# Another order for a program's opening: tables, norm rows and the first token tile ahead of the weight work

## What is computed

```python
def rms_norm(x, g):
    y = x * rsqrt(mean(x * x, axis=-1, keepdims=True) + EPS)
    return y * g
def swiglu(x, w_in, w_out):                # d_model 1024, d_ff 2816
    gate, up = split(x @ w_in, 2, axis=-1)
    return (silu(gate) * up) @ w_out
h = swiglu(rms_norm(x, g[0]), w_ffn_in[0, 0], w_ffn_out[0, 0])
x = x + 0.5 * rms_norm(h, g[1])
...
ATTN_PATTERNS = ((128, 1), (512, 4), (2048, 16))   # window, dilation: allowed distances
```

## Time and profile before

| | |
|---|---|
| median of 3 executions | 1462.7 us (1462.68 to 1465.63) |
| the profiled execution | time 1466.29 us, span 1464.4 us |
| granted TensorE clock, mean | 0.979 |
| TensorE products busy | 1389.5 us, 95% of the span |
| VectorE, ScalarE, GpSimd busy | 495.7, 659.1, 1037.0 us |
| DMA | 246.94 MB, mean 169 GB/s |

### The profile page before, as it was taken

The page is one execution under the profiler, slowest core; times in us unless marked ns, Lnnn a source line. Parts: engine busy times, 40 slices in busy tenths (PEclk is TensorE's granted clock), DMA queues, the critical chain, the costliest instruction groups (busy, mean ns, idle before and its releaser), DMA issues.

```text
span 1464.4 us, 17488 instructions
## 1 busy us (share of the span) xinstructions
PE 1389.5 (95%) x6396; PEld 1136.8 (78%) x6396; DVE 495.7 (34%) x1108; ACT 659.1 (45%) x760; POOL 1037.0 (71%) x241
## 2 busy tenths in 40 slices
PE   6799999989999999999999789999999999989997
PEld 4588888777888878888887567888878777778786
DVE  5610124565110156211003675110156133572235
ACT  5344435436444445544434556343455443544531
POOL 5778885818978866888887408978866966658763
PEclk9899999999999999999999989999999999999999
DMA  8555554515665554565655405556554644436541
GB/s 260 172 181 186 183 190 158 181 62 188 193 195 186 184 174 166 185 217 173 192 180 201 134 1 182 188 191 199 173 180 150 199 149 141 141 118 205 191 144 51
DMA packets 160668, 246.94 MB, mean 169 GB/s; under 512 B 8892, under 2 KB 99812, under 8 KB 160484
## 3 DMA queue, kind: packets, MB, share of 16 engines
q1 hardware_dynamic: 158180, 238.90, 49.9%
q10 hardware_dynamic: 2432, 7.28, 1.4%
HBM read 245.10 MB, written 1.05 MB: 168 GB/s over the span
## 4 chain that ended last, share of the span: by engine, by line
PE 36%; POOL 33%; issue 23%; DVE 5%; ACT 1%; DMA 1%; POOLq 1%; SPq 0%; ACTq 0%; DVEq 0%
POOL w_lo L502 33%; PE acc L1583 6%; PE acc L1585 6%; PE acc L1584 6%; PE gu L1583 3%; PE gu L1584 3%; PE gu L1585 3%; PE acc L1610 1%; PE acc L1616 1%; PE acc L1613 1%; PE gu L1958 1%; ACT w_hi L533 1%; DMA w_raw<-in_w_ffn_in 1%; PE tb L1967 1%; PE tb L1583 0%
## 5 line engine op out<-in xcount | busy, mean ns | idle before, releaser
L502 POOL TENSOR_TENSOR w_lo<-w_raw,w_hi 128x2048 fp32r<-128x2048 f32 x224 | 1031.5, 4623 | 396.2 <-ACT w_hi L533 389.0
L533 ACT CAST w_hi<-w_raw 128x2048 fp32r<-128x2048 f32 x226 | 425.9, 1907 | 78.7 <-PE gu L1585 20.8
L1583 PE MATMUL gu<-w_hi,xT_hi 128*128 128x512 f32 x832 | 331.7, 399 | 3.4 <-DVE xT_lo L1015 3.4
L1584 PE MATMUL gu<-w_lo,xT_hi 128*128 128x512 f32 x832 | 326.2, 392 | 0.0
L1585 PE MATMUL gu<-w_hi,xT_lo 128*128 128x512 f32 x832 | 326.1, 392 | 0.0
L1583 PE MATMUL acc<-w_hi,xT_hi 128*128 128x512 f32 x544 | 220.6, 406 | 3.7 <-DVE xT_lo L1015 2.7
L1585 PE MATMUL acc<-w_hi,xT_lo 128*128 128x512 f32 x544 | 214.8, 395 | 0.0
L1584 PE MATMUL acc<-w_lo,xT_hi 128*128 128x512 f32 x544 | 214.3, 394 | 0.0
L1583 PEld LDWEIGHTS gu<-w_hi,xT_hi 128*128 128x128 f32 x832 | 157.8, 190 | 35.4 <-issue 3.6
L1585 PEld LDWEIGHTS gu<-w_hi,xT_lo 128*128 128x128 f32 x832 | 157.6, 189 | 33.7
L1584 PEld LDWEIGHTS gu<-w_lo,xT_hi 128*128 128x128 f32 x832 | 158.0, 190 | 31.5 <-issue 0.2
(11 more groups left out here) (299 smaller groups left out, 1258.5 us busy)
## 6 DMA issues: line engine op xcount, KB each, us to landing
w_raw<-in_w_ffn_in SPq DMA_DIRECT2D x176, 512.0 KB, 4.7
w_raw<-in_w_ffn_out SPq DMA_DIRECT2D x88, 512.0 KB, 4.2
w_raw<-in_w_in SPq DMA_DIRECT2D x80, 512.0 KB, 4.5
w_raw<-in_mlstm_w_in SPq DMA_DIRECT2D x24, 512.0 KB, 4.3
w_raw<-in_w_ple_gate SPq DMA_DIRECT2D x16, 512.0 KB, 4.3
w_raw<-in_w_kv SPq DMA_DIRECT2D x16, 512.0 KB, 4.4
w_raw<-in_mlstm_w_out SPq DMA_DIRECT2D x8, 512.0 KB, 4.3
w_raw<-in_diff_w_q SPq DMA_DIRECT2D x8, 512.0 KB, 4.0
```

What stands on the lines that cost most here:

```text
L502: pool.tensor_tensor(w_lo[:, slot.spl, :], w_raw[:, slot.raw, :], w_hi[:, slot.spl, :].bitcast(F32), ALU.subtract).then_inc(lo_ready, 1)
L533: nc.scalar.copy(w_hi[:, slot.spl, :], w_raw[:, slot.raw, :]).then_inc(hi_ready, 1)
L1583: mm(out, xh, wh, start=(half == 0 and k == 0), stop=False)
L1584: mm(out, xh, wl, start=False, stop=False)
```

## The change

The opening is written in another order; the amount of matrix work stays.

- GpSimd runs the two iotas first, with a semaphore of their own; the other constants follow.
- VectorE builds the tables as its first work, with 10 operations instead of 13 (a compare and an add, a compare and a product, and a compare and a scaling are each one operation).
- ScalarE's DMA queue has the norm rows first, then token tile 0. Token tile 1 moves to SyncE's queue, between slots 0 and 1.
- ScalarE rounds tile 0's columns first, then slot 0 in four quarters with a signal for each; slot 2 now comes after tile 1's columns.
- VectorE subtracts slot 0 in four quarters after tile 0's columns; GpSimd has no part of slot 0 any more. SyncE no longer waits for half of slot 0.
- TensorE transposes only tile 0 at first, takes slot 0 quarter by quarter for tile 0, and transposes tile 1 between slots 0 and 1.

```diff
--- before.py
+++ after.py
@@ -240,7 +240,9 @@
 
         raw_landed = [sem(f"raw_landed{i}") for i in range(NRAW)]
         hi_ready = sem("hi_ready")
-        lo_half_ready = sem("lo_half_ready")
+        first_hi_part = sem("first_hi_part")
+        first_lo_part = sem("first_lo_part")
+        iota_ready = sem("iota_ready")
         lo_ready = sem("lo_ready")
         tile0_used = sem("tile0_used")
         slot_used = sem("slot_used")
@@ -260,7 +262,6 @@
         ht_hi_ready = sem("ht_hi_ready")
         ht_lo_ready = sem("ht_lo_ready")
         consts_ready = sem("consts_ready")
-        tables_ready = sem("tables_ready")
         gain_landed = sem("gain_landed")
         rows1_landed = sem("rows1_landed")
         rows2_landed = sem("rows2_landed")
@@ -390,9 +391,10 @@
 
             def load(slot, halves):
 
+                if slot.turn is None and slot.s == 1:
+                    sp.dma_start(x[:, 1, :], A["x"][0, tok(1), :]).then_inc(x_landed[1], 16)
                 if slot.turn is None and slot.s == NRAW:
                     small_loads()
-                    sp.wait_ge(lo_half_ready, 1)
                 if slot.turn is not None or slot.s >= NRAW:
 
                     sp.wait_ge(lo_ready, slot.count(-NRAW))
@@ -475,16 +477,16 @@
         @block.gpsimd
         def _(pool):
 
+            pool.iota(iota_i[:, 0:P], pattern=[[-1, P]], base=256, channel_multiplier=1).then_inc(iota_ready, 1)
+            pool.iota(iota_i[:, P:LCOLS], pattern=[[-1, 2 * P]], base=256 + P,
+                      channel_multiplier=1).then_inc(iota_ready, 1)
             pool.memset(ident[:], 0.0).then_inc(consts_ready, 1)
             pool.memset(causal[:], 0.0).then_inc(consts_ready, 1)
             pool.memset(upto[:], 1.0).then_inc(consts_ready, 1)
             pool.memset(ones[:], 1.0).then_inc(consts_ready, 1)
             pool.memset(last_row[:], 0.0).then_inc(consts_ready, 1)
 
-            pool.iota(iota_i[:, 0:P], pattern=[[-1, P]], base=256, channel_multiplier=1).then_inc(consts_ready, 1)
-            pool.iota(iota_i[:, P:LCOLS], pattern=[[-1, 2 * P]], base=256 + P,
-                      channel_multiplier=1).then_inc(consts_ready, 1)
-            pool.wait_ge(consts_ready, 7)
+            pool.wait_ge(consts_ready, 5)
             pool.affine_select(out=ident[:], in_=ident[:], compare_op=ALU.not_equal, fill=1.0, base=0,
                                pattern=[[-1, P]], channel_multiplier=1).then_inc(consts_ready, 1)
             pool.affine_select(out=causal[:, 0:P], in_=causal[:, 0:P], compare_op=ALU.is_ge, fill=FAR, base=0,
@@ -503,9 +505,6 @@
                                    w_hi[:, slot.spl, :].bitcast(F32), ALU.subtract).then_inc(lo_ready, 1)
 
 
-            pool.wait_ge(hi_ready, 1)
-            pool.tensor_tensor(w_lo[:, 0, 0:SLOT // 2], w_raw[:, 0, 0:SLOT // 2],
-                               w_hi[:, 0, 0:SLOT // 2].bitcast(F32), ALU.subtract).then_inc(lo_ready, 1)
             pool.wait_ge(lo_ready, 2)
             for s in range(2, NSPL):
                 subtract(At(s))
@@ -897,19 +896,22 @@
                     sum_of(FINAL_SUM, t, x[:, t, :])
 
 
+            act.dma_start(rows1, A["norm_g"].rearrange("l n (k c) -> (l n k) c", c=P)).then_inc(rows1_landed, 16)
             act.dma_start(x[:, 0, :], A["x"][0, tok(0), :]).then_inc(x_landed[0], 16)
-            act.dma_start(rows1, A["norm_g"].rearrange("l n (k c) -> (l n k) c", c=P)).then_inc(rows1_landed, 16)
-            act.dma_start(x[:, 1, :], A["x"][0, tok(1), :]).then_inc(x_landed[1], 16)
-            act.wait_ge(consts_ready, 12)
+            act.wait_ge(consts_ready, 10)
             warm(ACT.Silu)
-            round_hi(At(0))
             t_hi("F0", 0)
+            act.wait_ge(raw_landed[0], At(0).raw_count())
+            for part in range(4):
+                cols = slice(512 * part, 512 * part + 512)
+                nc.scalar.copy(w_hi[:, 0, cols], w_raw[:, 0, cols]
+                               ).then_inc(first_hi_part if part < 3 else hi_ready, 1)
             round_hi(At(1))
+            pre_sum("F0", 0)
+            t_hi("F0", 1)
             round_hi(At(2))
-            t_hi("F0", 1)
-            pre_sum("F0", 0)
+            pre_sum("F0", 1)
             round_hi(At(3))
-            pre_sum("F0", 1)
             p_hi(0)
             act.wait_ge(wg_landed, 32)
             nc.scalar.copy(wg_hi[:], wg_raw[:]).then_inc(wg_split, 1)
@@ -1097,8 +1099,6 @@
 
                 for n in range(2):
                     iteration(n, None)
-                    if n == 0 and name == "F0":
-                        build_tables()
                 with dve.Fori(0, (NIT - 3) // 2) as i:
                     for d in (0, 1):
                         iteration(2 + d, i)
@@ -1496,23 +1496,18 @@
 
             def build_tables():
 
-                dve.wait_ge(consts_ready, 12)
-                fdist, m4, m16, fwin = (build[:, i, :] for i in range(4))
+                dve.wait_ge(iota_ready, 2)
+                fdist, m4, m16 = (build[:, i, :] for i in range(3))
                 v.tensor_scalar(iand_i[:, 0:LCOLS], iota_i, 3, None, ALU.bitwise_and)
                 v.tensor_scalar(iand_i[:, LCOLS:2 * LCOLS], iota_i, 15, None, ALU.bitwise_and)
                 link(v.tensor_scalar(fdist, iota_i, -256.0, None, ALU.add))
                 v.tensor_scalar(m4, iand_i[:, 0:LCOLS], 0.0, None, ALU.is_equal)
-                v.tensor_scalar(m16, iand_i[:, LCOLS:2 * LCOLS], 0.0, None, ALU.is_equal)
-                link(v.tensor_scalar(fwin, fdist, float(P), None, ALU.is_le))
+                link(v.tensor_scalar(m16, iand_i[:, LCOLS:2 * LCOLS], 0.0, None, ALU.is_equal))
                 link(v.tensor_tensor(m4, m4, m16, ALU.add))
-                link(v.tensor_tensor(m4, m4, fwin, ALU.add))
-                link(v.tensor_scalar(m16, fdist, 0.0, None, ALU.is_ge))
-                link(v.tensor_tensor(times[:], m4, m16, ALU.mult))
-
-                link(v.tensor_scalar(m4, times[:], 0.5, None, ALU.is_le))
-                link(v.tensor_scalar(m4, m4, FAR, None, ALU.mult))
-                v.tensor_tensor(rel[:], m4, fdist, ALU.subtract).then_inc(tables_ready, 1)
-                dve.wait_ge(tables_ready, 1)
+                link(v.scalar_tensor_tensor(m4, fdist, float(P), m4, ALU.is_le, ALU.add))
+                link(v.scalar_tensor_tensor(times[:], fdist, 0.0, m4, ALU.is_ge, ALU.mult))
+                link(v.tensor_scalar(m4, times[:], 0.5, FAR, ALU.is_le, ALU.mult))
+                link(v.tensor_tensor(rel[:], m4, fdist, ALU.subtract))
 
             def first_lo(slot):
                 dve.wait_ge(hi_ready, slot.count())
@@ -1520,14 +1515,20 @@
                                 w_hi[:, slot.spl, :].bitcast(F32), ALU.subtract).then_inc(lo_ready, 1)
 
 
+            build_tables()
             dve.wait_ge(gcol_in_psum, 1)
             v.tensor_copy(gcol[:, 0:P], acc[:, 0, 0:P]).then_inc(gcol_ready, 1)
             dve.wait_ge(gcol_ready, 1)
 
-            dve.wait_ge(hi_ready, 1)
-            v.tensor_tensor(w_lo[:, 0, SLOT // 2:], w_raw[:, 0, SLOT // 2:],
-                            w_hi[:, 0, SLOT // 2:].bitcast(F32), ALU.subtract).then_inc(lo_half_ready, 1)
             t_units("F0", 0)
+            for part in range(4):
+                cols = slice(512 * part, 512 * part + 512)
+                if part < 3:
+                    dve.wait_ge(first_hi_part, part + 1)
+                else:
+                    dve.wait_ge(hi_ready, 1)
+                v.tensor_tensor(w_lo[:, 0, cols], w_raw[:, 0, cols], w_hi[:, 0, cols].bitcast(F32), ALU.subtract
+                                ).then_inc(first_lo_part if part < 3 else lo_ready, 1)
             dve.wait_ge(lo_ready, 1)
             first_lo(At(1))
             t_units("F0", 1)
@@ -1571,12 +1572,17 @@
 
                 pe.wait_ge(t_lo_ready, 4 * T[q] + 2 * t + half + 1)
 
-            def across_tile(slot, half, t, out, q=None):
-
-                pe.wait_ge(lo_ready, slot.count())
+            def across_tile(slot, half, t, out, q=None, by_part=False):
+
+                if not by_part:
+                    pe.wait_ge(lo_ready, slot.count())
                 if q:
                     has_t(q, t, half)
                 for k in range(4):
+                    if by_part and k < 3:
+                        pe.wait_ge(first_lo_part, k + 1)
+                    elif by_part:
+                        pe.wait_ge(lo_ready, 1)
                     wh = w_hi[:, slot.spl, 512 * k:512 * k + 512]
                     wl = w_lo[:, slot.spl, 512 * k:512 * k + 512]
                     xh, xl = xT_hi[:, 4 * half + k, tok(t)], xT_lo[:, 4 * half + k, tok(t)]
@@ -1676,7 +1682,15 @@
                 if name == "F2":
                     t_of_x(name, 1)
 
-                by_tile(s0, 2, name, lambda c, t: gu[:, t, :], (second_tile, None))
+                if name == "F0":
+                    across_tile(At(0), 0, 0, gu[:, 0, :], name, by_part=True)
+                    t_of_x(name, 1)
```

(10 more changed lines are left out.)

## The result

The changed kernel takes 1450.75 us (median of four executions, 1449.65 to 1450.99) against 1463.81 for the kernel before in the same runs; ratio 0.9908, 95% interval 0.9892 to 0.9924. It is faster, by some 11 to 16 us. The forecast was 1445.0 with a range of 1442.5 to 1450.0: right in sign, too large in size, and the median lies 0.75 us above the range.

A forecast was written before the change was run, and what follows sets the result against it. It took TensorE as the bound, held up by table operations at 40 to 60 us and by the opening's order. 13.5 + 4.2 = 17.7 us, taken from the median 1462.7, gave 1445.0, range 1442.5 to 1450.0.

The forecast's parts named there:

- The opening's term: From the program's start to slot 2 on TensorE: start at 26.4 us in place of 30.58, gaining 4.2 us.
- The stall's term: TensorE's idle time before hidden chunk 1's transposes, and the low clock behind it, go: 13.5 us.
- tile 1's columns: Before slot 2, VectorE scales token tile 1 from 16.2 us and ScalarE has rounded it at 18.1.
- What follows the columns: ScalarE rounds slot 2 to 20.0 us, L607 ends at 25.9, the gate product at 26.4, starting TensorE's slot 2.
- the tile's landing: Token tile 0's load in the opening: lands at 6.3 us, with 7.4 as the bound on the other side.
- the gain is the same in both: The shown median, 1462.7, is 3.6 us below the profiled time; the 17.7 us gain holds for both, giving 1445.0.
- B: Opening gives little, chunk 0's gate only 0 to 2 us earlier; time 1447.2 to 1449.2; chance 0.17.
- A: As summed, with the opening worth 2.5 to 5.5 us: 1443.5 to 1446.7, forecast 1445.0; chance 0.55.
- slot 3's landing: An example within B, in the opening: slot 3's buffer lands after ScalarE wants it at 21.2 us.
- C: At the start, VectorE's tables collide with GpSimd's constants and end at 8.9 us; 1.5 us less, 1446.5; chance 0.12.
- D: GpSimd's first subtraction after 21.1 us uses up 1.1 us of slack at chunk 1; 1446 to 1448; chance 0.10.
- E: TensorE's clock stays at the lower level; at 128 products 7.9 us slower, 1470.6; chance 0.03.

The follow-up runs named there:

- the tables alone: Kernel before, with iotas first on GpSimd and the ten-operation tables as VectorE's first work; median 1450.36 us.
- the second execution: The kernel after run and profiled once more without an edit; median 1449.53 us, ratio 0.9891 to the kernel before.
- tile 1 early: Kernel after, with token tile 1's eight transposes ahead of slot 0's products on TensorE; median 1446.95 us.
- three-edit kernel: Kernel after, with tile 1's transposes before slot 0's products, slot 2 rounded before tile 1's columns, VectorE's 128x64 gate-weight operation behind iteration 0; 1448.90 us.
- the warmed one: Three-edit kernel with ScalarE's first SiLU ahead of slot 4's rounding, plus eight unneeded TensorE products ahead of the gain transpose; median 1446.53 us.
- the opening alone: Kernel after, with the ten-operation tables back behind iteration 0 in VectorE's queue; median 1462.78 us, ratio 0.9986 to the kernel before.

## Why the median moved less than the trace: the clock of the later stages

The kernel with the tables alone had a lead 2.2 us smaller than the kernel after at 73 us, and the same median; in the profiled executions it even ended 1.5 us ahead (16.8 against 15.3), at a mean clock of 0.986 against 0.982. What differs after that, as far as the stretches show, is TensorE's clock. The busy time by stretch of the kernel after, and then of the kernel with the tables alone (PEclk is the third number from the end):

```profile
240.00:260.00 20.00, 17.36 (x69) 13.02 (x68) 16.56 (x18) 6.07 (x9) 16.19 (x4) 0.91 0.59 202
...
520.00:540.00 20.00, 17.70 (x75) 14.37 (x74) 12.32 (x37) 11.42 (x16) 9.18 (x2) 0.91 0.44 154
```

```profile
240.00:260.00 20.00, 17.14 (x74) 13.15 (x73) 15.84 (x13) 7.73 (x8) 18.44 (x4) 1.00 0.49 160
...
520.00:540.00 20.00, 17.70 (x83) 14.50 (x82) 13.34 (x39) 13.01 (x17) 9.18 (x2) 1.00 0.41 144
```

The same code with the same pauses between stages drops to the lower level in one execution and not in the other. It is so within one kernel too: the four executions with the tables alone had spans of 1446.9, 1447.6, 1449.4 and 1453.0 us at mean clocks of 0.987, 0.986, 0.984 and 0.982. Some 6 us lie between them, more than the whole reordering of the opening brings. What decides whether a pause costs the clock was not tested, so it stays open.

## Why the prediction was off, by its own steps

The error is 5.75 us (1450.75 against 1445.0), and it has two parts that can be told apart.

**The opening's term, 2.4 us.** From the profiled execution of before the sum gives 1466.3 - 17.7 = 1448.6; the profiled one of after took 1450.99. The stall's term of 13.5 us is right: the lead grows by 13.47 between slot 2 and the way down, in the whole change and with the tables alone. The opening's 4.2 us measured 1.9, and 2.9 in the second execution. The step that failed is the one of tile 1's columns. The prediction let VectorE scale them at 16.2, straight behind slot 1's low part, and had itself written beside it that TensorE is done with slot 0 and tile 1's transposes at 15.6 to 18.1. It took the lower end without a reason. All twelve products started at the lower clock's pace (12.22 to 17.05, 0.43 us each), the transposes came behind them, and VectorE began the columns at 18.38. What follows the columns was forecast rightly: from there to slot 2's first product it reckoned 10.2 us, and the kernel after took 10.3 in both executions, the kernel with tile 1 early 10.4. So nearly all of the 2.3 us lies ahead of the columns: 1.4 us VectorE waited for tile 1's transposes (0.7 in the second execution, none with them moved), and 0.8 us slot 1's low part was late (ending at 17.0 in place of 16.2; 16.7 in the second execution), behind the tile's landing at 7.4, which the text had as its bound. The second execution has 1.3 of the 2.3; the first execution's other 1.0 is that landing, spread over both.

**The step "the gain is the same in both", 3.4 us.** The profiled execution of before was 3.6 us above the median of the three shown, and this was carried over as a constant. For after the two differ by 0.2 us. The 3.6 was chance on both sides: the median of the three lay 1.9 below that of the 29 later executions, 1464.6, and the profiled one 1.7 above it. From 1464.6 the same sum gives 1446.9, and with the measured lead of 15.4 to 16.4 us 1448.2 to 1449.2; the rest to 1450.75 is within what the later stages' clock moves.

The rivals: *B* came true in size for the opening (1.9 us; in the second execution 2.9, which is *A*'s size), and one of its examples came with it in the first execution, the tile's landing at 7.4. Its other one, slot 3's landing, bounds nothing until the chain is 2 us shorter (21.0 us in the three-edit kernel), where it does; and tile 1's transposes it doesn't name. Its whole time, 1447.2 to 1449.2, still lies below the median. *C* is in the rows (constants end at 5.93 in place of 3.89, the tables at 6.37, not 8.9), at no cost. *D*'s slack held: gate products at 43.5 to 44.4, transposes at 45.6. *E* didn't come. One slip is in *A*: an opening worth 5.5 us gives 1443.7, not 1443.5, which moves nothing else. The range was too narrow because it took the opening's terms at their middle and put 1 us for the spread; the executions of before alone scatter from 1461.0 to 1466.9.

## What to carry to other kernels

On this kernel a block of small VectorE operations beside GpSimd's long ones cost by the number of operations that meet one and by how much of it is left, not by their size: four table operations of 128x384 elements took 4.1 to 4.8 us each, and one of 128x64 took 3.5, or 0.8 where it met the end. Put such work where GpSimd stands still or where nothing waits behind it. After each reordering ask what stands next in the queue of the slowest chain: here the SiLU stood behind two roundings that nobody needed yet, and moving one call gave 1.2 us. A wait of TensorE can cost the clock on top of its length, 1.6 us behind one of 2.3 here. And compare executions product by product before trusting a difference of a few microseconds in medians.

## What was not expected of the hardware

In the first 18 us the granted clock stands at 1.00 in the stretches of all kernels but the warmed one, while slot 0's first products start 0.43 us apart. In the warmed one its first products do so too, and there the stretch from 10 to 12 us is recorded at 0.50. So in these traces the record ahead of its first fall doesn't tell the level; the pace does. GpSimd's selects on 128x128 elements took 0.43 to 0.64 us beside VectorE's tables and 0.29 to 0.30 without them (the kernel with the opening alone), while the tables' own operations stayed near their unhindered 0.35 and 0.56. In that meeting GpSimd paid, and with the long subtractions VectorE does.
